# Gathering rows for a mixture of experts in two parts of 256 slots, with expert 0's products between the parts

## The chip, the cores and the metric

The kernel runs on one core of one Trainium2 chip. The metric is the device time of one execution in microseconds (us); lower is better. The core's engines are TensorE (PE, whose weight loads are listed as PEld), VectorE (DVE), ScalarE (ACT), GpSimd (POOL) and SyncE (SP), which here does little but issue transfers (DMA) from the chip's memory in its program order.

## The reference

A trunk of two layers over 256 tokens of width 1024, in float32. Each layer has a mixer (retention and chunked attention in layer 0, sliding-window attention in layer 1), then a hierarchical mixture of experts, then a gated embedding. What the change touches is the mixture:

```
g = argmax(group logits)            # one of 4 groups
top 2 of the 4 experts inside it    # 16 experts in all, two per token
act = silu(h @ w_gate[e]) * (h @ w_up[e]) * gate   # d_ff 512
out += act @ w_down[e]              # for the tokens that chose e
```

With two experts per token there are 512 token-expert pairs. Each expert has three matrices of 2 MB, 96 MB for a layer.

## The kernel before

**The mixture.** Pairs are sorted by expert into 512 slots. VectorE builds one-hot matrices PH (`gather_onehots`, tokens x slots; lines 1971 to 1974) from the slot numbers, and TensorE multiplies the normalised rows by them, which writes the rows, turned, in slot order. The rows are split in a high and a low part (HSP, `rows_split`), so that two products of a fast type give the accuracy of one. For each of the 8 steps k of the width there are 2 token tiles x 2 parts = 4 matmuls of 512 columns (line 983), 32 in a layer. The stationary operand is `HSP[part][:, t, k:D:KD]`, read with a stride of 8 elements. ScalarE and VectorE copy each product, scaled by the norm's weight, out of PSUM to XS (lines 1501, 1991). Expert e takes 64 slots from its offset on, copied to XE (`expert_rows`).

**An expert** is gate and up (`gate_up`, line 1024: 8 steps k of two matmuls, which the trace shows as 32 records; the first half is k below 4), the activation, a turn back (line 1033), down (line 1041, 16 records), and the scatter of its output with one-hots again (line 1049). From expert 2 on `step(e)` runs gate and up of e, then down of e - 1. If an expert has more than 64 rows a loop behind reloads its weights; it is not taken here.

**The order ahead of that.** In each layer TensorE gathers k = 0 to 3 of token tile 0, opens the second pair of sums (`open_sums`), gathers k = 0 to 3 of tile 1, runs the first halves of experts 0 and 1 (`first_rows`), gathers k = 4 to 7, then expert 0's second half (`other_rows(0)`), the spreads of slot numbers and gates (lines 1010 and 1012), and expert 1's second half. For expert 0 the first four k have small copies of their own of the first 64 slots (`first_block`).

**The transfers.** Weights go through nine slots of 2 MB (`weights`). A load into a slot waits for the products that read it before: halves are counted by `gate_up_halves` and `gate_up_ready`, `y_halves` and `y_ready`. All weight loads are issued by SyncE in one written order, so a load that waits holds up those behind it. The eight loads of 1 MB that follow the first three experts stand in this order for both halves:

```
for half in range(2):
    load_part(3, 1, half)   # slot of expert 0's gate
    load_part(4, 0, half)   # slot of expert 0's up
    load_part(4, 1, half)   # slot of expert 1's gate
    load_part(3, 2, half)   # slot of expert 1's up
```

Experts in WHOLE (6 to 13) load gate and up in one transfer of 2 MB each, the others in halves. Between the loads SyncE also stores the side product (the embedding's projection, `side_half_stored`) and fetches expert 2's down weight to places outside the nine slots (XD, and H by `outside`).

Of the kernel before, what the change touches and what calls it, by code (L numbers as in the profile page):

```python
# [15 lines left out]
D = 1024  # L16
# [38 lines left out]
WHOLE = (6, 14)  # L55
# [132 lines left out]
def rows_bank(k):  # L188

    return (0, 1, 4, 5, 1, 4, 1, 4)[k]  # L190
# [20 lines left out]
def build(nc, x, p, norm_mix, norm_ffn, norm_ple, final_norm, even_w_in, even_ret_gn, even_rel_bias, even_w_out,  # L211
# [6 lines left out]
    with ExitStack() as ctx:  # L218
# [196 lines left out]
        def _(sp):  # L415
# [30 lines left out]
            def experts(l, u0):  # L446
# [51 lines left out]
                for e in range(NE):  # L498
                    if e == 3:
# [173 lines left out]
        def _(pe):  # L673
# [224 lines left out]
            def experts(l, u0):  # L898
# [81 lines left out]
                def gathered_part(k, t):  # L980

                    for part in range(2):
                        mm = pe.matmul(B[rows_bank(k)][:, :], HSP[part][:, t, k:D:KD], PH[:, t, :], start=(t + part == 0),  # L983
                                       stop=(t + part == TT))
                    if t == 1:
                        mm.then_inc(sem("rows_ready"), 1)

                def gathered_first(t):

                    pe.wait_ge(sem("onehots_ready"), 2 * l + t + 1)  # L990
                    pe.wait_ge(sem("hs_low"), 3 * l + 1 + t)
                    pe.wait_ge(sem("side_copied"), 4 * l + 2)
                    for k in range(4):
                        gathered_part(k, t)

                def gathered(k, t):

                    pe.wait_ge(sem("hs_low"), 3 * l + 3)
                    if t == 0:
                        name, steps = (("rows_by_dve", 1), ("rows_by_act", 2), ("rows_by_act", 3), ("rows_by_dve", 3))[k - 4]  # L1000
                        pe.wait_ge(sem(name), 4 * l + steps)
                    gathered_part(k, t)

                def spread():

                    pe.wait_ge(sem("gates_ready"), l + 1)
                    pe.wait_ge(sem("rows_by_act"), 4 * (l + 1))
                    pe.wait_ge(sem("rows_by_dve"), 4 * (l + 1))
# [130 lines left out]
                def first_block(k):  # L1139

                    if k < 4:
                        pe.wait_ge(sem("first_block_by_dve" if k % 2 else "first_block_by_act"), 2 * l + k // 2 + 1)
                    else:
                        pe.wait_ge(sem("rows_by_dve" if k % 2 else "rows_by_act"), 4 * l + k // 2 + 1)

                def first_rows(e):

                    n = u0 + 3 * e
                    if e == 0:
                        pe.wait_ge(sem("rows_by_act"), 4 * l + 1)  # L1150
                    else:
                        pe.wait_ge(sem("xe_first"), l + 1)
                        pe.wait_ge(sem("rows_by_dve"), 4 * l + 2)
                    wait_unit(n)
                    wait_unit(n + 1)
                    gate_up(B[gu_bank(e)], XE[:, e], pair(n), None, sem("gate_up_halves"), (0,),
                            first_block if e == 0 else None)

                def other_rows(e):

                    n = u0 + 3 * e
                    if e == 1:
                        pe.wait_ge(sem("xe_ready"), NE * l + 2)
                    gate_up(B[gu_bank(e)], XS[:, :, 0:BLK] if e == 0 else XE[:, e], pair(n), lambda: wait_second(n, n + 1), None, (1,),
                            first_block if e == 0 else None).then_inc(sem("gate_up_ready"), 1)
# [12 lines left out]
                other_rows(1)  # L1178
# [189 lines left out]
        def _(act):  # L1368
# [92 lines left out]
            def experts(l, u0):  # L1461
# [21 lines left out]
                for half in range(2):  # L1483
                    seed(1, half)
# [9 lines left out]
                def first_block(k):  # L1494

                    act.wait_ge(sem("rows_ready"), 8 * l + k + 1)
                    act.activation(XE[:, 0, k], B[rows_bank(k)][:, 0:BLK], ACT.Copy, scale=NW[:, kn, k:k + 1])\
                        .then_inc(sem("first_block_by_act"), 1)

                def rows_evac(k):  # L1500
                    act.activation(XS[:, k, :], B[rows_bank(k)][:, :], ACT.Copy, scale=NW[:, kn, k:k + 1]).then_inc(sem("rows_by_act"), 1)
# [3 lines left out]
                if l == 1:  # L1505
                    act.wait_ge(sem("gate_up_ready"), NE * l - 1)
                for half in range(2):
                    for k in (4 * half, 4 * half + 2):
                        if half == 0:
                            first_block(k)  # L1510
                        else:
                            act.wait_ge(sem("rows_ready"), 8 * l + k + 1)
                        if k == 0:
                            act.wait_ge(sem("side_first_stored"), 16 * (l + 1))
                        rows_evac(k)
                    act.wait_ge(sem("rows_by_act"), 4 * l + 2 * half + 2)
                    act.wait_ge(sem("rows_by_dve"), 4 * l + 2 * half + 2)
                    rows(1, offs, slice(4 * half, 4 * half + 4), ("xe_first", "xe_ready")[half], (1, 2)[half])
                    if half == 0:
                        act.wait_ge(sem("g_below_max"), l + 1)  # L1520
                        act.activation(RT[:, 20:28], RT[:, 20:28], ACT.Exp).then_inc(sem("g_exp"), 1)
                        act.wait_ge(sem("second_below_first"), l + 1)
                        act.activation(RT[:, 84:86], RT[:, 84:86], ACT.Exp).then_inc(sem("second_exp"), 1)
# [157 lines left out]
        def _(dve):  # L1681
# [186 lines left out]
            def experts(l, u0):  # L1868
# [102 lines left out]
                for t in range(TT):  # L1971
                    then(dve.tensor_scalar(TMP[:, t, :], IOTA, S2[:, t, :], None, ALU.is_equal))
                    dve.scalar_tensor_tensor(out=PH[:, t, :], in0=IOTA, scalar=S1[:, t, :], in1=TMP[:, t, :],
                                             op0=ALU.is_equal, op1=ALU.add).then_inc(sem("onehots_ready"), 1)
# [6 lines left out]
                rows_low(1, 4, KD)  # L1981

                def first_block(k):

                    dve.wait_ge(sem("rows_ready"), 8 * l + k + 1)
                    dve.tensor_scalar(XE[:, 0, k], B[rows_bank(k)][:, 0:BLK], NW[:, kn, k:k + 1], None, ALU.mult)\
                        .then_inc(sem("first_block_by_dve"), 1)

                def rows_evac(k):

                    dve.tensor_scalar(XS[:, k, :], B[rows_bank(k)][:, :], NW[:, kn, k:k + 1], None, ALU.mult).then_inc(sem("rows_by_dve"), 1)

                if l == 1:
                    dve.wait_ge(sem("gate_up_ready"), NE * l - 1)
                first_block(1)
                dve.wait_ge(sem("side_first_stored"), 16 * (l + 1))
                rows_evac(1)
                first_block(3)
                dve.wait_ge(sem("side_second_stored"), 16 * (l + 1))
                rows_evac(3)  # L2000
# [67 lines left out]

                dve.wait_ge(sem("rows_ready"), 8 * l + 6)
                rows_evac(5)  # L2070
                dve.wait_ge(sem("rows_ready"), 8 * l + 8)
                dve.wait_ge(sem("side_third_stored"), 16 * (l + 1))
                rows_evac(7)
# [308 lines left out]
```

## Time and profile before

| | |
|---|---|
| time, median of 3 runs | 727.9 us (726.28 to 727.92) |
| the profiled execution's own time | 727.73 us |
| its span | 725.9 us |
| TensorE busy | 706.7 us, 97% |
| VectorE, ScalarE busy | 301.5 us, 166.1 us |
| transfers | 250.87 MB, mean 346 GB/s |
| granted clock of TensorE, mean | 0.994 |

In rows of windows the columns are the stretch and its length; the busy us and (in brackets) instructions of PE, PEld, DVE, ACT and POOL; the granted clock of TensorE; the share of the transfer engines; and GB/s. In rows of a timeline they are start, length to the end of the last, engine, line, operation, operands and count, and in square brackets the idle time before it and what ended that. The span is the time between the first and the last instruction of the profiled execution; 1.8 us lie around it. Each engine runs its own list of instructions and waits on semaphores. A busy engine need not be what sets the time: what counts is which wait ends last at the end of each stage.

### The profile page before, as it was taken

What the parts mean: (1) busy time and instruction counts of PE and PEld (TensorE: products, weight loads), DVE (VectorE), ACT (ScalarE), POOL (GpSimd) and SP (SyncE); (2) the same over time, 40 slices, a digit from 0 to 9 for tenths busy, and PEclk for the clock granted to TensorE, in tenths of its full rate; (3) what the DMA queues carried; (4) which work ended last, traced back from release to release, by engine and by line L of the source; (5) the groups of instructions that cost most, each with busy time, mean ns of one, the idle gap of its engine ahead of it and who ended that gap; (6) DMA issues with size and microseconds to landing.
All of it is one profiled execution on the core that took longest, in us unless ns stands there. A gap on an engine that the chain in (4) does not pass through costs nothing.

```text
span 725.9 us, 8170 instructions
## 1 busy us (share of the span) xinstructions
PE 706.7 (97%) x3062; PEld 328.4 (45%) x3062; DVE 301.5 (42%) x717; ACT 166.1 (23%) x395; POOL 26.4 (4%) x47
## 2 busy tenths in 40 slices
PE   9999999999999999989999999999999999989996
PEld 5488454564333333333445545455333333333344
DVE  1213361545437343433322557263535534324324
ACT  3000241432111111110331144252111111112132
POOL 0500000000000000000000000000000000000000
PEclk9999999999999999999999999999999999999999
DMA  9998448889999999999999851489999999999941
GB/s 344 376 285 293 184 174 328 331 310 367 421 409 424 424 431 424 426 418 422 398 381 409 328 197 79 180 284 355 412 412 426 429 422 424 428 420 422 406 164 59
DMA packets 46056, 250.87 MB, mean 346 GB/s; under 512 B 4200, under 2 KB 5448, under 8 KB 25536
## 3 DMA queue, kind: packets, MB, share of 16 engines
q1 hardware_dynamic: 43648, 245.04, 84.4%
q0 software_dynamic: 2048, 5.07, 2.2%
q8 instruction: 26, 0.43, 0.2%
q10 hardware_dynamic: 320, 0.22, 0.1%
q14 instruction: 14, 0.11, 0.0%
HBM read 247.15 MB, written 4.73 MB: 347 GB/s over the span
## 4 chain that ended last, share of the span: by engine, by line
PE 81%; DMA 9%; SPq 5%; issue 2%; DVE 2%; ACT 1%; POOLq 0%; POOL 0%; ACTq 0%; DVEq 0%
PE bank L1024 25%; PE bank L699 24%; PE bank L1041 12%; SPq L454 4%; DMA weights<-in_moe_w_up_dram 4%; PE bank L732 4%; DMA weights<-in_moe_w_down_dram 4%; PE bank L1049 3%; PE bank L983 2%; PE bank L926 2%; PE bank L684 1%; PE bank L1033 1%; DMA weights<-in_even_w_in_dram 1%; PE bank L712 1%; PE bank L770 0%
## 5 line engine op out<-in xcount | busy, mean ns | idle before, releaser
L1024 PE MATMUL bank<-weights,expert_rows 128*64 128x512 f32 x992 | 222.5, 600 | 6.2 <-DMA weights<-in_moe_w_up_dram 6.2
L699 PE MATMUL bank<-weights,normalised 128*128 128x512 f32 (+1 forms) x448 | 191.4, 580 | 0.9 <-DVE normalised L1699 0.7
L1024 PEld LDWEIGHTS bank<-weights,expert_rows 128*64 128x64 f32 x992 | 73.7, 138 | 147.1 <-issue 145.8
L699 PEld LDWEIGHTS bank<-weights,normalised 128*128 128x128 f32 x448 | 83.1, 190 | 91.4 <-issue 88.5
L1041 PE MATMUL bank<-weights,hidden_turned_odd 128*64 128x512 f32 x256 | 58.8, 598 | 0.4 <-DMA weights<-in_moe_w_down_dram 0.4
L1041 PE MATMUL bank<-weights,hidden_turned 128*64 128x512 f32 x224 | 51.5, 598 | 1.3 <-DVE hidden_turned L2029 0.6
L1534 ACT ACTIVATE gate_tanh<-bank 128x256 f32<-128x256 f32 x32 | 12.3, 384 | 175.2 <-PE bank L1024 175.2
L1385 ACT ACTIVATE expert_outputs<-bank 64x512 fp32r<-64x512 f32 (+1 forms) x32 | 18.9, 591 | 117.7 <-PE bank L1041 112.3
L2029 DVE COPY hidden_turned<-bank 128x256 f32<-128x256 f32 x16 | 6.8, 424 | 75.0 <-PE bank L1033 75.0
L2060 DVE TENSOR_TENSOR expert_outputs<-bank,expert_outputs 64x512 fp32r<-64x512 f32 x30 | 20.5, 684 | 41.7 <-ACT expert_outputs L1385 41.5
L2029 DVE COPY hidden_turned_odd<-bank 128x256 f32<-128x256 f32 x16 | 6.8, 424 | 63.3 <-PE bank L1033 63.1
L1041 PEld LDWEIGHTS bank<-weights,hidden_turned_odd 128*64 128x64 f32 x256 | 16.9, 136 | 34.8 <-issue 31.7
L2041 DVE SCALAR_TENSOR_TENSOR spread_gates<-token_slots,router_temps,token_gates 128x512 f32<-128x512 f32 x32 | 24.0, 751 | 12.9 <-ACT token_gates L1526 11.9
L1041 PEld LDWEIGHTS bank<-weights,hidden_turned 128*64 128x64 f32 x224 | 15.2, 136 | 29.2 <-issue 28.9
L732 PE MATMUL bank<-normalised,weights 128*128 128x256 f32 x128 | 28.4, 380 | 0.0
L1049 PE MATMUL bank<-expert_outputs,scatter_onehots 128*128 128x512 f32 x60 | 26.1, 436 | 0.2
L732 PEld LDWEIGHTS bank<-normalised,weights 128*128 128x128 f32 x128 | 24.1, 190 | 3.7 <-issue 0.5
L1049 PE MATMUL bank<-gather_onehots,scatter_onehots 128*128 128x512 f32 x60 | 23.6, 394 | 0.0
L2044 DVE TENSOR_REDUCE slot_gates<-spread_gates 128x1 f32<-128x512 f32 x32 | 21.9, 686 | 1.1
L1385 ACT ACTIVATE expert_rows<-normalised 128x512 f32 (+1 forms) x32 | 19.5, 611 | 10.9 <-issue 6.9
L1033 PEld LDWEIGHTS bank<-constants,hidden 128*128 128x128 f32 x64 | 10.1, 206 | 26.3 <-issue 24.7
L1381 ACT ACTIVATE normalised<-bank,norm_weights 128x128 f32<-128x128 f32 x48 | 13.7, 368 | 33.3 <-PE bank L684 33.0
(276 smaller groups left out, 647.1 us busy)
## 6 DMA issues: line engine op xcount, KB each, us to landing
weights<-in_moe_w_down_dram SPq DMA_DIRECT2D x60, 1024.0 KB, 19.6
weights<-in_moe_w_gate_dram SPq DMA_DIRECT2D x32, 1024.0 KB, 8.7
weights<-in_moe_w_up_dram SPq DMA_DIRECT2D x32, 1024.0 KB, 10.1
weights<-in_moe_w_gate_dram SPq DMA_DIRECT2D x16, 2048.0 KB, 16.5
weights<-in_moe_w_up_dram SPq DMA_DIRECT2D x16, 2048.0 KB, 21.0
weights<-in_even_w_in_dram SPq DMA_DIRECT2D x5, 2048.0 KB, 20.4
weights<-in_ple_w_gate_dram SPq DMA_DIRECT2D x4, 2048.0 KB, 31.5
weights<-in_even_w_out_dram SPq DMA_DIRECT2D x2, 2048.0 KB, 32.5
```

Source lines behind the costliest of these rows:

```text
L454: sp.dma_start(dst, src).then_inc(done, 16)
L699: mm = pe.matmul(B[bank][:, 0:width], XT[:, k, tok(t)], w[:, k, :], start=(k == 0), stop=(k == KD - 1))
L732: mm = pe.matmul(B[2 * (u % 2) + pair][:, c * SEQ:(c + 1) * SEQ], w[:, k, tok(2 * pair + c)], XT[:, k, :], start=(k == 0), stop=(k == KD - 1))
L926: mm = pe.matmul(B[4 + 2 * t + half][:, :], PINT[:, k, tok(t)], WPL[k][:, half * 512:(half + 1) * 512], start=(k == 0), stop=(k == 1))
L1024: mm = pe.matmul(bank[j * BLK:(j + 1) * BLK, :].rearrange("p (m f) -> p m f", m=2), rows[:, k, :], W[:, slots, a:a + FF // 2], start=(k == ...
L1033: mm = pe.transpose(B[TURNED_BANK][:, c * P:(c + 1) * P], US[:, c:2 * P:2], ident)
L1041: mm = pe.matmul(bank[half * BLK:(half + 1) * BLK, :], hid[:, 2 * (f % 2) + f // 2, :], rows(f)[:, half * 512:(half + 1) * 512], start=(f ...
L1049: return pe.matmul(B[sum_bank(t, half)][:, :], PT2[:, par, tok(t)], YSPLIT[half][:, par, :], start=False, stop=stop)
L1385: return act.activation(dst, src, ACT.Copy)
L2041: stepped(dve.scalar_tensor_tensor(out=SPREAD, in0=SROW.rearrange("p c s -> p (c s)"), scalar=col, in1=WROW.rearrange("p c s -> p (c s)"), ...
L2044: stepped(dve.tensor_reduce(GATES[:, par:par + 1], SPREAD, AX.X, ALU.add), gates)
L2060: return dve.tensor_tensor(YSPLIT[half][low, par, :], bank[high, :], YSPLIT[half][high, par, :].bitcast(F32), ALU.subtract)
```

## The change

The gather is divided by slots instead of by k. First TensorE gathers slots 0 to 255 for all eight k (32 matmuls of 256 columns), then runs expert 0's whole gate and up, reading its rows from XS, then gathers slots 256 to 511 (32 more), then expert 1's first half, the spreads, and expert 1's second half. Two k share a PSUM bank. The one-hots are built for 256 slots at a time, with the low part of the rows of tile 1 between. `first_block` goes. ScalarE copies k = 0, 1, 4, 5 and VectorE k = 2, 3, 6, 7 of each part, 256 wide. ScalarE seeds the second pair of sums behind its first two copies. SyncE stores the last quarter of the side product ahead of the 1 MB load of expert 2's down weight, not behind it. WHOLE becomes 8 to 13, so experts 6 and 7 load gate and up in halves, in the branch `elif e != 4`: first halves of both, then second halves, then down of the expert before. The order of the other loads is as it was.

```diff
-WHOLE = (6, 14)
+WHOLE = (8, 14)
...
-def rows_bank(k):
-    return (0, 1, 4, 5, 1, 4, 1, 4)[k]
+def rows_bank(half, k):
+    return ((0, 1, 4, 5), (5, 4, 1, 4))[half][k // 2]
+def in_bank(k):
+    return slice(256 * (k % 2), 256 * (k % 2) + 256)
+def evac_count(half, k):
+    return 4 * half + 2 * (k // 4) + k % 2 + 1
...
# SyncE
                         side_half_stored(0)
-                        sp.wait_ge(sem("side_ready"), 4 * l + 4)
+                        sp.wait_ge(sem("side_copied"), 4 * l + 4)
+                        side_half_stored(1)
                         sp.dma_start(XD[:, :], srcs[2][l * NE + 2][0:256, :].rearrange("(p c) d -> p (c d)", c=2))\
                             .then_inc(sem("down2_landed"), 16)
-                        sp.wait_ge(sem("side_copied"), 4 * l + 4)
-                        side_half_stored(1)
...
# TensorE
+                def gathered(half, k):
+                    for t in range(TT):
+                        for part in range(2):
+                            mm = pe.matmul(B[rows_bank(half, k)][:, in_bank(k)], HSP[part][:, t, k:D:KD],
+                                           PH[:, t, 256 * half:256 * half + 256], start=(t + part == 0), stop=(t + part == TT))
+                    mm.then_inc(sem("rows_ready"), 1)
+                def gathered_first():
+                    pe.wait_ge(sem("onehots_ready"), 4 * l + 2)
+                    pe.wait_ge(sem("hs_low"), 3 * l + 2)
+                    pe.wait_ge(sem("side_copied"), 4 * l + 2)
+                    for k in range(4):
+                        gathered(0, k)
+                    pe.wait_ge(sem("side_copied"), 4 * l + 4)
+                    open_sums(1)
+                    pe.wait_ge(sem("hs_low"), 3 * l + 3)
+                    for k in range(4, KD):
+                        gathered(0, k)
+                def gathered_second():
+                    pe.wait_ge(sem("onehots_ready"), 4 * l + 4)
+                    for k in range(KD):
+                        if k == 0:
+                            pe.wait_ge(sem("rows_by_dve"), 8 * l + evac_count(0, 7))
+                        elif k == 2:
+                            pe.wait_ge(sem("rows_by_act"), 8 * l + evac_count(0, 5))
+                        elif k == 6:
+                            pe.wait_ge(sem("rows_by_dve"), 8 * l + evac_count(1, 3))
+                        gathered(1, k)
...
-                gathered_first(0)
-                pe.wait_ge(sem("side_copied"), 4 * l + 4)
-                open_sums(1)
-                gathered_first(1)
-                first_rows(0)
-                first_rows(1)
-                for k in range(4, KD):
-                    for t in range(TT):
-                        gathered(k, t)
-                other_rows(0)
+                gathered_first()
+                first_expert()
+                gathered_second()
+                second_expert(0)
                 spread()
-                other_rows(1)
+                second_expert(1)
...
# ScalarE
+                act.wait_ge(sem("side_first_stored"), 16 * (l + 1))
+                rows_evac(0, 0)
+                rows_evac(0, 1)
+                for half in range(2):
+                    seed(1, half)
+                act.wait_ge(sem("onehots_ready"), 4 * l + 4)
+                rows_evac(0, 4)
+                rows_evac(0, 5)
...
+                for part in range(2):
+                    rows_evac(1, 4 * part)
+                    rows_evac(1, 4 * part + 1)
+                    act.wait_ge(sem("rows_by_act"), 8 * l + evac_count(1, 4 * part + 1))
+                    act.wait_ge(sem("rows_by_dve"), 8 * l + evac_count(1, 4 * part + 3))
+                    rows(1, offs, slice(4 * part, 4 * part + 4), ("xe_first", "xe_ready")[part], (1, 2)[part])
...
# VectorE
+                gather_onehots(0)
+                rows_low(1, 4, KD)
+                gather_onehots(1)
...
+                rows_evac(0, 2)
                 dve.wait_ge(sem("side_second_stored"), 16 * (l + 1))
-                rows_evac(3)
+                rows_evac(0, 3)
+                rows_evac(0, 6)
+                dve.wait_ge(sem("side_third_stored"), 16 * (l + 1))
+                rows_evac(0, 7)
...
+                for k in (2, 3, 6, 7):
+                    rows_evac(1, k)
```

## Rows read from the trace of the kernel before

**Rows 1.** The page: TensorE busy, and the transfers' share by slice

```profile
PE 706.7 (97%) x3062; PEld 328.4 (45%) x3062; DVE 301.5 (42%) x717; ACT 166.1 (23%) x395; POOL 26.4 (4%) x47
...
DMA  9998448889999999999999851489999999999941
```

**Rows 2.** Waits of TensorE: us in total, times, longest

```profile
PE bank L1024 <- DMA weights<-in_moe_w_up_dram: 6.2, 4, 2.7
```

**Rows 3.** Windows: engines' busy us, granted clock, transfers' share, GB/s

```profile
210.00:222.00 12.00, 12.00 (x58) 4.34 (x56) 5.08 (x11) 2.20 (x4) 0.00 (x0) 1.00 0.97 410
...
246.00:258.00 12.00, 12.00 (x58) 4.32 (x56) 5.04 (x11) 2.21 (x4) 0.00 (x0) 1.00 1.01 425
...
310.00:314.00 4.00, 2.66 (x8) 0.92 (x10) 0.73 (x2) 0.00 (x0) 0.00 (x0) 0.65 1.01 420
```

**Rows 4.** Timeline of TensorE, ends of both layers' experts: start, length in us

```profile
311.34 8.71 PE L1024 MATMUL bank<-weights,expert_rows 128*64 128x512 f32 x32 [2.72 <-DMA weights<-in_moe_w_up_dram]
...
351.34 1.94 PE L1041 MATMUL bank<-weights,hidden_turned_odd 128*64 128x512 f32 x8 [0.42 <-DMA weights<-in_moe_w_down_dram]
...
682.53 3.85 PE L1041 MATMUL bank<-weights,hidden_turned_odd 128*64 128x512 f32 x16
```

**Rows 5.** Timeline of TensorE, layer 0, from the first gather

```profile
146.74 2.51 PE L983 MATMUL bank<-gather_onehots,rows_split 128*128 128x512 f32 x8
...
151.87 7.09 PE L1024 MATMUL bank<-weights,expert_rows 128*64 128x512 f32 x32
...
158.89 4.69 PE L983 MATMUL bank<-gather_onehots,rows_split 128*128 128x512 f32 x16
...
163.50 3.65 PE L1024 MATMUL bank<-weights,normalised 128*64 128x512 f32 x16
...
169.07 3.65 PE L1024 MATMUL bank<-weights,expert_rows 128*64 128x512 f32 x16
```

**Rows 6.** Timeline of SyncE's queue (SPq), loads of experts 3 and 4

```profile
155.56 0.33 SPq L454 DMA_DIRECT2D weights<-in_moe_w_up_dram  x1
...
159.00 0.33 SPq L454 DMA_DIRECT2D weights<-in_moe_w_up_dram  x1
...
167.20 0.33 SPq L454 DMA_DIRECT2D weights<-in_moe_w_up_dram  x1
...
172.76 0.33 SPq L454 DMA_DIRECT2D weights<-in_moe_w_up_dram  x1
...
492.64 0.33 SPq L454 DMA_DIRECT2D weights<-in_moe_w_up_dram  x1
```

**Rows 7.** Windows of 22 and of 2 us, same columns

```profile
154.00:176.00 22.00, 21.20 (x100) 10.78 (x98) 8.94 (x26) 4.90 (x10) 0.00 (x0) 1.00 0.86 326
...
696.00:698.00 2.00, 2.00 (x6) 0.95 (x5) 0.15 (x1) 1.64 (x5) 0.09 (x1) 1.00 0.50 207
```

**Rows 8.** Timeline of the weight loads (PEld), in short windows

```profile
147.14 1.80 PEld L983 LDWEIGHTS bank<-gather_onehots,rows_split 128*128 128x128 f32 x7
...
158.88 0.31 PEld L983 LDWEIGHTS bank<-gather_onehots,rows_split 128*128 128x128 f32 x1 [0.81 <-issue]
...
159.10 0.59 PEld L983 LDWEIGHTS bank<-gather_onehots,rows_split 128*128 128x128 f32 x2
```

**Rows 9.** Groups by line: count, busy us, mean ns of one

```profile
L983 PEld LDWEIGHTS bank<-gather_onehots,rows_split 128*128 128x128 f32 x64 | 16.5, 329 | 3.3 <-issue 2.4 <-DVE gather_onehots L1973 0.5
...
L1049 PEld LDWEIGHTS bank<-expert_outputs,scatter_onehots 128*128 128x128 f32 x60 | 11.5, 192 | 3.4 <-issue 2.2
```

**Rows 10.** The chain that ended last: start us, us, what

```profile
184.96 0.93 PE bank L1049 x4
...
379.42 0.88 PE bank L684 x8
```

**Rows 11.** Timeline of VectorE, the slots' selection, layer 0

```profile
145.37 0.49 DVE L1972 TENSOR_SCALAR normalised<-normalised,router_temps 128x512 f32<-128x512 f32 x1
...
147.07 0.75 DVE L1973 SCALAR_TENSOR_TENSOR gather_onehots<-normalised,router_temps 128x512 fp32r<-128x512 f32 x1
```

More of the change, by code:

```diff
@@ L978, in experts @@
                 side_part(1, 1, 1)
[L980 to L991, printed above, removed]
+                def gathered(half, k):
[4 more added lines that the diff above has]
+                    mm.then_inc(sem("rows_ready"), 1)
@@ L1170, in experts, with row_in_place, first_expert @@
-                gathered_first(1)
-                first_rows(0)
-                first_rows(1)
-                for k in range(4, KD):
-                    for t in range(TT):
-                        gathered(k, t)
-                other_rows(0)
+                def row_in_place(k):
+                    pe.wait_ge(sem("rows_by_act" if by_act(k) else "rows_by_dve"), 8 * l + evac_count(0, max(k, 1)))
+                def first_expert():
+                    wait_unit(u0)
+                    wait_unit(u0 + 1)
+                    gate_up(B[gu_bank(0)], XS[:, :, 0:BLK], pair(u0), lambda: wait_second(u0, u0 + 1), sem("gate_up_halves"),
+                            row_ready=row_in_place).then_inc(sem("gate_up_ready"), 1)
@@ new lines, in second_expert @@
+                def second_expert(half):
+                    n = u0 + 3
+                    if half == 0:
+                        pe.wait_ge(sem("xe_first"), l + 1)
+                        pe.wait_ge(sem("rows_by_act"), 8 * l + evac_count(1, 1))
+                        wait_unit(n)
+                        wait_unit(n + 1)
+                        gate_up(B[gu_bank(1)], XE[:, 1], pair(n), None, sem("gate_up_halves"), (0,))
+                    else:
+                        pe.wait_ge(sem("xe_ready"), NE * l + 2)
+                        gate_up(B[gu_bank(1)], XE[:, 1], pair(n), lambda: wait_second(n, n + 1), None, (1,))\
+                            .then_inc(sem("gate_up_ready"), 1)
@@ L1482, in experts @@
                             seed(0, half)
-                for half in range(2):
-                    seed(1, half)
                 def rows(e, off=None, part=slice(0, KD), done="xe_ready", count=1):
@@ L1492, in rows, with rows_evac @@
                     copy(XE[:, e % 2, part], XS[:, part, bass.ds(off, BLK)]).then_inc(sem(done), count)
[L1494 to L1501, printed above, removed]
+                def rows_evac(half, k):
+                    act.wait_ge(sem("rows_ready"), 16 * l + 8 * half + k + 2 - k % 2)
+                    act.activation(XS[:, k, 256 * half:256 * half + 256], B[rows_bank(half, k)][:, in_bank(k)], ACT.Copy,
+                                   scale=NW[:, kn, k:k + 1]).then_inc(sem("rows_by_act"), 1)
@@ new lines, in experts @@
+                act.wait_ge(sem("side_first_stored"), 16 * (l + 1))
[6 more added lines that the diff above has]
+                rows_evac(0, 5)
+                act.wait_ge(sem("g_below_max"), l + 1)
+                act.activation(RT[:, 20:28], RT[:, 20:28], ACT.Exp).then_inc(sem("g_exp"), 1)
+                act.wait_ge(sem("second_below_first"), l + 1)
@@ L1503, in experts @@
+                act.activation(RT[:, 84:86], RT[:, 84:86], ACT.Exp).then_inc(sem("second_exp"), 1)
                 act.wait_ge(sem("table_ready"), 2 * l + 1)
                 offs = act.value_load(TBL[0:1, 1:2], min_val=0, max_val=LAST)
[L1505 to L1523, printed above, removed]
@@ L1970, in experts, with gather_onehots @@
                 dve.wait_ge(sem("iota_ready"), 2 * (l + 1))
[L1971 to L1974, printed above, removed]
+                def gather_onehots(half):
+                    c = slice(256 * half, 256 * half + 256)
+                    for t in range(TT):
+                        then(dve.tensor_scalar(TMP[:, t, c], IOTA[:, c], S2[:, t, :], None, ALU.is_equal))
+                        dve.scalar_tensor_tensor(out=PH[:, t, c], in0=IOTA[:, c], scalar=S1[:, t, :], in1=TMP[:, t, c],
+                                                 op0=ALU.is_equal, op1=ALU.add).then_inc(sem("onehots_ready"), 1)
+                gather_onehots(0)
+                rows_low(1, 4, KD)
+                gather_onehots(1)
                 one = slice(0, 1)
```

54 lines of the change are left out of this document (8 added, 46 removed).

## The prediction

> **What bounds the kernel now.** I read the page first. TensorE is busy 97% of the span, and the transfers run at nine tenths or more in most slices [rows 1], so shares alone decide nothing. The waits of TensorE for transfers sum to only 6.2 us in four waits [rows 2]. Read alone, that says TensorE is the bound. The windows and the timeline say otherwise for the expert stretches. From about 174 us to the end of layer 0's experts the transfers move 410 to 425 GB/s at a share of 0.97 to 1.01 [rows 3], and at the end TensorE waits 0.42 us for the second half of the last down weight before it can do the last 8 matmuls at 351.34 [rows 4]. An expert takes TensorE some 11.8 us and the transfers 3 x 2.10 MB at 0.424 MB/ns, 14.8 us. TensorE eats up a lead of filled slots, starts to wait at the twelfth expert or so, and the layer ends when its last weight lands. That is a chain of transfers that runs without a gap back to about 173 us. So the question for the change is what it does to the transfers in the 30 us ahead of that, where the queue still runs dry: 154 to 176 us moved 326 GB/s [rows 7].
>
> What starts transfers there? SyncE issues in program order, and each of four pairs of 1 MB waits for a slot: pair A for expert 0's first half of gate and up, pair B for expert 1's first half, pair C for expert 0's second half, pair D for expert 1's second. They go at 155.6, 159.0, 167.2 and 172.8 [rows 6]. The timeline of TensorE shows the causes: first halves of experts 0 and 1 together from 151.87 to 158.9, then gathers, expert 0's second half from 163.50, then the spreads, expert 1's second half from 169.07 [rows 5].
>
> **The change part by part.**
>
> *Gathers, 32 of 512 columns become 64 of 256 in each layer.* The price is the spacing of such matmuls. Now seven weight loads of the gather take 1.80 us, the last 0.33: (1.80 - 0.33)/6 = 0.245 us from one to the next [rows 8]. The scatters, also 128x512 out of fp32r operands, are spaced at 0.93/4 = 0.232 [rows 10]. The difference lies in the load: 0.330 us each in the gather, whose stationary rows are read at a stride of 8, against 0.192 in the scatter [rows 9]. And after a gap, with no matmul streaming, the gather's first load starts at 158.88 and its second at 159.10 [rows 8]: 0.22 us for a load by itself. So the gather's spacing today is the load's, not the 512 columns', and half the columns save next to nothing. I take 0.24; bounds are 0.22 (a bare load) and 0.245, and as the far end 0.11, at which the transposes of 128 columns run (0.87/8) [rows 10], if the load turned out to be no limit. At 0.24, 32 gathers are 7.7 us.
>
> The Trainium skill, in "TensorE: Matmul & The Clock Gate", section "LDWEIGHTS (loading the stationary operand)", gives a load as its columns over 1.2, 107 ns for 128, and its section "Back-to-back issue gap" gives 256 columns 109 ns. By the page's figures 32 gathers would be 3.5 us and the whole about 731 us. By that rule, the trace disagrees: 0.22 to 0.245 us lie between its loads.
>
> *The order.* The start stays: the side product holds TensorE until 147.1 [rows 8]. Selecting the slots takes VectorE from 145.37 to 147.8 now for both token tiles [rows 11]; half as wide, four operations take between half of that and all of it, so the gather starts between 147.1 and 147.8; I take 147.1. Then:
> first gather 7.7, and 0.4 for opening two sums: 155.2;
> expert 0 whole, twice the 3.5 us of 16 matmuls [rows 5]: 162.2, its first half at 158.7;
> second gather 7.7 and 0.2 for its first load: 170.1;
> expert 1's first half 3.6: 173.7;
> spreads 2.0, second half 3.6: 179.3.
> Today expert 1's first half ends at 158.9, the spreads at 169.1 and its second half at 172.7 [rows 5]. So expert 0 is whole 5 us earlier (167.1 to 162.2), its first half 3.3 us later, expert 1's first half 14.8 us later and its second 6.6 later. TensorE alone is 6.6 us later from here on, 7.7 of gathers less some gaps.
>
> *The transfers.* Pair A goes at 158.8. Pair B must wait for 173.7, and pair C, free since 162.2, stands behind it in SyncE's queue. It then goes at once, D at 179.3. Pair A lands within some 1.5 us (issue to data) plus 2.10/0.424 = 4.9 us, at about 165, and then nothing moves for 9 us. From 173.7 on the queue stays full, as it does now from 172.8. But at that point today A, B and C are done, and then only A is. The transfers are behind by two pairs and 0.9 us: 2 x 4.9 + 0.9 = 10.8 us. A little of it can come back where they run below their best today (410 against 425 GB/s in 210 to 222 us [rows 3], 0.4 us): 10.4.
>
> *What hides it.* Nothing at layer 0's end: TensorE already waits there [rows 4], so the end moves by 10.4. TensorE's own 6.6 us lie inside. What was some 3.1 us of waits in the layer, half of the 6.2, becomes about 7. An idle stretch also lowers the clock: 310 to 314 us has a granted clock of 0.65 [rows 3] after the 2.72 us wait, a mix of 2.4 and 1.2 GHz, and the 32 matmuls there take 8.71 us [rows 4] for 7.0. There is room for that under 14.8 us an expert, so I cost it at nothing, 1.7 us where the cover fails at the last expert.
>
> Layer 1 has the same order at an offset of 333.6 us (pair B at 492.64 [rows 6]) and pays the same 10.4. At its end the last 16 matmuls run without a wait [rows 4], so there is slack. The transfers end at about 697 [rows 7]; after the last down weight come 5.8 MB (two gates, side product, a row), 14 us, so it lands at 683.0 and its matmuls start at 684.4. Slack 1.4: layer 1 moves by 9.0.
>
> *The small parts.* Evacuations become 256 wide and twice as many. The eight of the first part lie beside the 7 us of expert 0, where ScalarE and VectorE have no other product to fetch; in the second part matmuls 6 and 7 reuse a bank that VectorE empties two copies (under 0.75 us each) before, beside 2 us of gathers; a stall of 0 to 1 us. The eight small copies of expert 0's rows go (under 0.3 us each, beside gathers): nothing. Seeding the second sums moves behind two evacuations, so the 0.5 MB load that waits for it goes about 1.6 us later, the 1 MB one 1 us later; both land before 158.8 in a queue that is dry anyway. Expert 6 and 7 in halves ask for each slot's half earlier; with the queue full that reorders bytes and starts nothing: 0, at best the 0.4 us above once more.
>
> **Sum.** 10.4 + 9.0 = 19.4 us on the profiled execution's 727.7 (span 725.9 and 1.8 around it): 747.1. That execution stands 0.2 below the median of the runs, 727.9. I say 747.
>
> **Rivals.**
> A, short gathers: the load is no limit at 256 columns, spacing 0.11. Then expert 1's first half ends at 158.4 + 64 x 0.11 = 165.4 and pair B is late by less; the lag is that end less 162.9 (173.7 less 10.8), 2.5 us, less the slack in layer 1: 2.5 + 1.1 = 3.6, 731 us. For it: half the columns. Against it: the 0.22 us between bare loads.
> B, the lag is partly made up: the transfers catch up and TensorE's 6.6 us set each end, less waits of today: 5 to 6 us a layer, 739. It needs 450 GB/s over 177 us; the windows show 425.
> C, the other side: pair C 5 us earlier wins. It decides only where pair B, ahead of it in SyncE's order, goes before 162.9, which needs a spacing under (162.9 - 158.4)/64 = 0.07 us. At 0.05, as for half the time of a 128-column transpose, the lag is -1.3 a layer: 725. No row has such a spacing.
> D, no effect: a spacing of about 0.07, 728.
>
> **Numbers.** My forecast 0.76, A 0.10, B 0.07, C 0.04, D 0.03. Its own range: spacing 0.22 takes 64 x 0.02 = 1.3 us a layer off, 744.5; start at 147.8, a stall of 1 us and a cold last expert in both layers put 0.7 + 1 + 0.5 a layer on, 751.5. With B the range is 738 to 752, which leaves A, C and D out. A difference under 0.3% (2.2 us) can't be told from none here. Faster 0.04, same 0.03, slower 0.93.
>
> **What would show it.** In the trace after: 128 gather matmuls spaced at 0.24 us with loads still of 0.33; in SyncE's timeline a single pair near 158.8 and then nothing until about 173.7, when four 1 MB loads go within 2 us; in the windows from 166 to 174 a transfer share near 0; TensorE's waits for transfers up from 6 us to about 14, the first at expert 11 or 12; the same in layer 1. Wrong it would be if the gathers' spacing fell to 0.12 (A), or if the lag at 174 us were not there any more at the last down weight (B).

## The result, and the profile after

| | before | after |
|---|---|---|
| time, median of 4 runs, taken in turn | 727.91 us (726.28 to 729.18) | 748.52 us (747.97 to 748.98) |
| the profiled execution's own time | 727.73 us | 748.98 us |
| its span | 725.9 us | 747.2 us |

The ratio is 1.028, with a 95% interval of 1.026 to 1.031: slower, by 20.6 us between the medians. The forecast was 747 us. Medians and ratios below leave out the few executions that stood far above the rest of their kernel (782.69 us once in 12, and 815 to 1871 us three times among those of the kernel before).

The page of the kernel after, its span, busy times, transfers in 40 slices, and the gather's groups:

```profile
span 747.2 us, 8320 instructions
PE 722.4 (97%) x3126; PEld 345.9 (46%) x3126; DVE 303.2 (41%) x729; ACT 167.2 (22%) x399; POOL 26.4 (4%) x47
DMA  9998349865999999999999760665999999999941
L998 PEld LDWEIGHTS bank<-gather_onehots,rows_split 128*128 128x128 f32 x128 | 31.2, 336 | 3.3 <-issue 2.1
L998 PE MATMUL bank<-gather_onehots,rows_split 128*128 128x256 f32 x128 | 32.4, 409 | 0.0
```

TensorE is busy 97% of a span that is 21 us longer: the share says nothing, as before [rows 1]. A load of the gather's stationary rows takes 336 ns, about as it did [rows 9], and there are twice as many. The slices, each 18.7 us long, show the place. In the ninth and tenth, 149 to 187 us, the transfers' share is six and five tenths, where the ninth and tenth of before, 145 to 181 us, have eight and nine [rows 1]. In layer 1 the 27th and 28th, 486 to 523 us, have six and five.

The timeline of TensorE, from the first gather in layer 0 (it answers to [rows 5]):

```profile
147.70 4.13 PE L998 MATMUL bank<-gather_onehots,rows_split 128*128 128x256 f32 x16
...
152.17 4.11 PE L998 MATMUL bank<-gather_onehots,rows_split 128*128 128x256 f32 x16
156.21 7.09 PE L1047 MATMUL bank<-weights,normalised 128*64 128x512 f32 x32
163.23 7.97 PE L998 MATMUL bank<-gather_onehots,rows_split 128*128 128x256 f32 x32
171.13 3.65 PE L1047 MATMUL bank<-weights,expert_rows 128*64 128x512 f32 x16
...
176.70 3.65 PE L1047 MATMUL bank<-weights,expert_rows 128*64 128x512 f32 x16
```

The second gather is 32 matmuls in 7.97 us; less the last one's 0.41 that is 7.56/31 = 0.244 us each. Expert 1's first half ends at 174.8.

SyncE's queue, the loads of experts 3 and 4 (it answers to [rows 6]):

```profile
159.91 0.33 SPq L469 DMA_DIRECT2D weights<-in_moe_w_up_dram  x1
...
174.83 0.33 SPq L469 DMA_DIRECT2D weights<-in_moe_w_up_dram  x1
...
175.67 0.43 SPq L469 DMA_DIRECT2D weights<-in_moe_w_up_dram  x1
...
180.39 0.33 SPq L469 DMA_DIRECT2D weights<-in_moe_w_up_dram  x1
...
503.50 0.33 SPq L469 DMA_DIRECT2D weights<-in_moe_w_up_dram  x1
...
518.42 0.33 SPq L469 DMA_DIRECT2D weights<-in_moe_w_up_dram  x1
```

Pair A stands alone at 159.91, pair B goes at 174.83, pair C right behind it, D at 180.39; layer 1 repeats it. The windows say what that costs (it answers to [rows 7]):

```profile
154.00:176.00 22.00, 22.00 (x101) 14.41 (x101) 5.52 (x25) 3.77 (x10) 0.00 (x0) 1.00 0.39 137
166.00:174.00 8.00, 8.00 (x36) 6.06 (x37) 1.75 (x4) 1.99 (x5) 0.00 (x0) 1.00 0.08 32
```

The stretch of 22 us moved 326 GB/s before and moves 137 now; in 166 to 174 us almost nothing is under way, while TensorE works without a gap.

The waits of TensorE for transfers, and its timeline at the ends of the layers (they answer to [rows 2] and [rows 4]):

```profile
PE bank L1047 <- DMA weights<-in_moe_w_up_dram: 11.4, 8, 2.7
...
PE bank L1064 <- DMA weights<-in_moe_w_down_dram: 0.9, 2, 0.5
```

```profile
292.63 7.09 PE L1047 MATMUL bank<-weights,expert_rows 128*64 128x512 f32 x32 [0.70 <-DMA weights<-in_moe_w_up_dram]
...
361.90 1.94 PE L1064 MATMUL bank<-weights,hidden_turned_odd 128*64 128x512 f32 x8 [0.47 <-DMA weights<-in_moe_w_down_dram]
...
705.71 1.94 PE L1064 MATMUL bank<-weights,hidden_turned_odd 128*64 128x512 f32 x8 [0.46 <-DMA weights<-in_moe_w_down_dram]
```

The sum is 12.3 us, the first wait of layer 0 is at expert 11 (292.63), and both layers now end on a wait for the last down weight. By stages, from the starts of such rows (us):

| stage | before | after | more |
|---|---|---|---|
| start to layer 0's first gather | 146.7 | 147.7 | 1.0 |
| to the last half of layer 0's last down | 204.6 | 214.2 | 9.6 |
| to layer 1's first gather | 129.1 | 129.4 | 0.3 |
| to the last half of layer 1's last down | 204.0 | 214.4 | 10.4 |
| to the end of the span | 41.4 | 41.4 | 0 |

### The profile page after: what moved, and what is told of

Same layout as the page of the kernel before. It is cut to its first block, busy times and chain, and to the rows that moved or that the text cites. A ratio compares the mean times of both kernels' runs of the same rounds, so it can differ in the third digit from the quotient of the medians.

```text
span 747.2 us, 8320 instructions
## 1 busy us (share of the span) xinstructions
PE 722.4 (97%) x3126; PEld 345.9 (46%) x3126; DVE 303.2 (41%) x729; ACT 167.2 (22%) x399; POOL 26.4 (4%) x47
## 4 chain that ended last, share of the span: by engine, by line
PE 69%; DMA 15%; SPq 10%; issue 2%; DVE 2%; ACT 1%; POOLq 0%; POOL 0%; ACTq 0%; DVEq 0%
PE bank L713 24%; PE bank L1047 17%; SPq L469 10%; DMA weights<-in_moe_w_up_dram 8%; PE bank L1064 7%; DMA weights<-in_moe_w_down_dram 7%; PE bank L998 4%; PE bank L746 4%; PE bank L940 2%; PE bank L1072 2%; PE bank L698 2%; PE bank L726 1%; PE bank L1056 1%; PE bank L852 1%; PE bank L784 0%
## 5 line engine op out<-in xcount | busy, mean ns | idle before, releaser
L1047 PE MATMUL bank<-weights,expert_rows 128*64 128x512 f32 x960 | 215.8, 601 | 11.4 <-DMA weights<-in_moe_w_up_dram 11.4
L1047 PEld LDWEIGHTS bank<-weights,expert_rows 128*64 128x64 f32 x960 | 72.7, 139 | 147.1 <-issue 146.6
L1542 ACT ACTIVATE gate_tanh<-bank 128x256 f32<-128x256 f32 x32 | 12.3, 384 | 181.3 <-PE bank L1047 181.3
L998 PEld LDWEIGHTS bank<-gather_onehots,rows_split 128*128 128x128 f32 x128 | 31.2, 336 | 3.3 <-issue 2.1
L998 PE MATMUL bank<-gather_onehots,rows_split 128*128 128x256 f32 x128 | 32.4, 409 | 0.0
L1399 ACT ACTIVATE expert_rows<-normalised 128x512 f32 (+1 forms) x32 | 19.5, 611 | 15.3 <-issue 10.9
```

The source lines that it names most:

```text
L998: mm = pe.matmul(B[rows_bank(half, k)][:, in_bank(k)], HSP[part][:, t, k:D:KD], PH[:, t, 256 * half:256 * half + 256], start=(t + part == ...
L1047: mm = pe.matmul(bank[j * BLK:(j + 1) * BLK, :].rearrange("p (m f) -> p m f", m=2), rows[:, k, :], W[:, slots, a:a + FF // 2], start=(k == ...
L1399: return act.activation(dst, src, ACT.Copy)
```

## Experiments

Each ratio is to the kernel before, run in turn with it on the same chip. Stages are read from one profiled execution each, and kernels that do the same in a stage differ there by up to 1.4 us.

### Only the wait, without the gathers

The kernel before, with pair B, and so all that stands behind it, held until the second half of expert 1 is done (`gate_up_ready` counts experts whose gate and up are whole):

```diff
                             load_part(4, 0, half)
+                            if half == 0:
+                                sp.wait_ge(sem("gate_up_ready"), NE * l + 2)
                             load_part(4, 1, half)
```

> The kernel before, with one wait added to SyncE: pair B waits for expert 1's second half (172.8 us in layer 0) instead of its first (159.0), so pairs B, C and D go together. TensorE gets no work. Theory 1, the chain of transfers sets each layer's end: at 174.3 us, when pair D's data starts now, two pairs are missing, 9.9 us; less 1.4 us of slack at the end of layer 1 the time is 727.9 + 9.9 + 8.5 = 746 us (743 to 748). Theory 2, TensorE's own 6.6 us per layer set the end of the changed kernel, and a gap in the transfers is made up before a layer ends: 728 us, at most 731.

744.61 us, ratio 1.025 (1.023 to 1.026). No instruction of TensorE was added or moved. SyncE's queue, the windows and the waits of this kernel:

```profile
155.66 0.33 SPq L454 DMA_DIRECT2D weights<-in_moe_w_up_dram  x1
...
172.84 0.33 SPq L454 DMA_DIRECT2D weights<-in_moe_w_up_dram  x1
```

```profile
154.00:176.00 22.00, 21.20 (x100) 10.77 (x98) 8.93 (x27) 4.90 (x10) 0.00 (x0) 1.00 0.39 135
...
200.00:230.00 30.00, 30.00 (x142) 10.63 (x140) 15.43 (x43) 5.59 (x10) 0.00 (x0) 1.00 1.01 425
```

```profile
PE bank L1026 <- DMA weights<-in_moe_w_up_dram: 19.3, 11, 2.7
```

At 172.84 pairs B, C and D go one behind another, where before only D was left: two pairs behind. That alone lengthens the expert stages by 8.1 and 8.9 us. So the stall of the transfers by itself makes a loss of nearly the size of the change's, and over 180 us little of it is caught up, where rival B wanted about half. TensorE, with less to do than in the kernel after, just waits longer: 19.3 us. The stall is not given back in full, but a little is: 9.8 us went in, 8.1 and 8.9 came out. From 200 to 230 us this kernel moves 425 GB/s where before moved 415 (its window is among those below): 0.7 us of that.

### Pair C ahead of pair B

The kernel after, with the pairs in the order in which their slots come free:

```diff
                         for half in range(2):
                             load_part(3, 1, half)
                             load_part(4, 0, half)
+                        for half in range(2):
                             load_part(4, 1, half)
                             load_part(3, 2, half)
```

> The changed kernel with pair C (free at about 163 us) issued ahead of pair B (free at about 175). TensorE's work is as in the changed kernel. Theory 1: one pair of 2.1 MB lands in the gap of the transfers, so the lag is 4.9 us less in each layer: 748.5 - 9.9 = 738.6 us (737 to 741). Theory 2: TensorE's added work is unchanged, so is the time: 748.5 us (747 to 750).

740.43 us, ratio 1.019 (1.017 to 1.021). SyncE's queue and two windows:

```profile
158.83 0.33 SPq L469 DMA_DIRECT2D weights<-in_moe_w_up_dram  x1
...
162.26 0.33 SPq L469 DMA_DIRECT2D weights<-in_moe_w_up_dram  x1
...
173.75 0.33 SPq L469 DMA_DIRECT2D weights<-in_moe_w_up_dram  x1
...
179.31 0.33 SPq L469 DMA_DIRECT2D weights<-in_moe_w_up_dram  x1
```

```profile
176.00:180.00 4.00, 3.75 (x18) 1.18 (x14) 3.02 (x7) 2.04 (x6) 0.00 (x0) 1.00 0.91 377
...
180.00:182.00 2.00, 1.44 (x8) 0.70 (x10) 1.93 (x5) 0.59 (x1) 0.00 (x0) 1.00 1.00 352
```

Pair C, which now goes 11.5 us ahead of pair B, wins 4.0 and 3.9 us in the two stages, about the 4.9 us of a pair. So 8 of the 20 us were the head of the queue: a load whose slot was free stood behind one whose slot was not. The rest of the 4.9: between B at 173.75 and D at 179.31 a single pair is under way, and the windows run at 377 and 352 GB/s, not 424, which is 0.4 + 0.3 us.

### What the gather's spacing is made of

Two ways to store the split rows so that the stationary operand is contiguous. In the first ScalarE and VectorE read the rows at a stride of 8; in the second they write them at a stride of 128 elements, and VectorE also reads the high part back at that stride. TensorE's line is the same in both. The edits are shortened here to VectorE's views; ScalarE's copy of the high part changes in the same way:

```diff
-  HSP[part][:, t, k:D:KD]
+  HSP[part][:, t, k * P:(k + 1) * P]
 # first: split kept as (k, m), rows read as (m, k)
+  cols      = lambda ap: ap.rearrange("p (k m) -> p k m", k=KD)[:, a:b, :]
+  wide_cols = lambda ap: ap.rearrange("p (m k) -> p k m", k=KD)[:, a:b, :]
 # second: rows read in order, split written as (m, k) into (k, m)
+  cols      = lambda ap: ap.rearrange("p (k m) -> p m k", k=KD)[:, :, a:b]
```

Contiguous, read at a stride, in the kernel after:

> The changed kernel, with the split rows stored in the order of k (written so by ScalarE and VectorE, read by the same count of elements), so that a gather's stationary operand is contiguous. Theory 1, the strided weight load spaces the gathers: the load falls from 0.33 to 0.19 us, the spacing from 0.25 to 0.12 or 0.13, expert 1's first half ends 8 us earlier, and the time is 731 to 735 us, 733 likeliest. Theory 3, a gather matmul costs 0.25 us for another reason (its issue, its type, the PSUM side): spacing and time stay, 748 us. If the strided reads in ScalarE and VectorE cost, the start of the gather is later by up to 1 us in each layer.

737.48 us, ratio 1.015 (1.013 to 1.018). The timeline of TensorE, and groups by line:

```profile
147.92 2.18 PE L998 MATMUL bank<-gather_onehots,rows_split 128*128 128x256 f32 x16
...
159.56 4.44 PE L998 MATMUL bank<-gather_onehots,rows_split 128*128 128x256 f32 x32
```

```profile
L998 PEld LDWEIGHTS bank<-gather_onehots,rows_split 128*128 128x128 f32 x128 | 15.8, 191 | 3.9 <-issue 2.1 <-DVE gather_onehots L1986 1.2 <-DVE normalised L2002 0.6
...
L1885 DVE SCALAR_TENSOR_TENSOR rows_split<-residual,norm_stats,rows_split 128x512 fp32r<-128x512 f32 (+1 forms) x6 | 8.9, 1478 | 8.5 <-ACT rows_split L1482 8.5
...
L1482 ACT ACTIVATE rows_split<-residual,norm_stats 128x1024 fp32r<-128x1024 f32 x4 | 8.6, 2161 | 0.0
```

The load falls from 336 to 191 ns and 32 matmuls from 7.97 to 4.44 us, 0.13 us each. The same 256 columns are now nearly half as dear: the stride in the load was the limit, not the columns. But the price goes elsewhere. ScalarE's pass over a tile of the rows rises from 1161 ns to 2161, VectorE's from 923 to 1478 on the mean, and the stage between the layers is 132.0 us, 2.9 more than before. Of the expert stages 2.2 and 2.6 us are left over before's. The time is 2.5 us above the range expected: the strided passes cost 1.2 us ahead of layer 0 and 2.9 between the layers, where up to 1 us a layer was allowed for.

Contiguous, written at a stride, the same kernel otherwise:

> The changed kernel with the split rows in the order of k by strided writes instead of strided reads. The stage between the layers took 132.0 us with strided reads against 129.1; the stages from the first gather to the last down product were 206.8 and 206.6. If writes at a stride are free: 129.1 between the layers and 737.5 - 4.2 = 733 us. If they cost the same: 737.5.

737.49 us, ratio 1.013 (1.011 to 1.015). ScalarE's pass takes 2.08 us: written or read at a stride, the price is the same.

The second way with pair C first:

> The changed kernel with both repairs: split rows in the order of k, this time read as they lie and written at a stride of 128 elements, and pair C issued ahead of pair B. By theory 1 the gathers are spaced at 0.13 us, pairs A, C, B, D go at about 155.5, 159, 167 and 172.5 us, against 155.6, 159.0, 167.2 and 172.8 for the four pairs of the kernel before: pair D's data starts 0 to 0.5 us earlier in each layer, 727 us (726 to 728.5), if the strided writes are free. If they cost as the strided reads did (3 us ahead of layer 1, 1.2 ahead of layer 0), 731 us.

730.35 us, ratio 1.004 (1.002 to 1.005). The expert stages are 203.4 and 204.4 us, those of before within what a stage varies; the 2.5 us left stand ahead of layer 0 (0.8) and between the layers (2.6), where the strided passes are, less the 0.8 gained in the expert stages.

### The 512-column gather with contiguous rows

The second way in the kernel before, nothing else changed:

> The kernel before, 512-column gathers, with the split rows in the order of k by strided writes. The spacing goes from 0.245 to the scatters' 0.232, set by the columns and no more by the load: 0.4 us a layer for TensorE, pairs C and D up to 0.3 us earlier, 726.5 us if the writes are free, about 731 if not. If the load were no limit at 512 columns either, the spacing would stay at 0.245.

730.46 us, ratio 1.004 (1.002 to 1.005): slower, though TensorE spends less on the gathers (16.5 us of loads become 11.4). The 16 gathers ahead of expert 0's second half take 4.29 us for 4.69 [rows 5]:

```profile
159.43 4.29 PE L983 MATMUL bank<-gather_onehots,rows_split 128*128 128x512 f32 x16
```

Between the starts of such matmuls lie 0.233 us for 0.247 (medians). So contiguous, 512 columns are spaced at 0.23 us and 256 at 0.13; at a stride of 8 both are at about 0.245. TensorE's timeline between the layers, of this kernel and then of before:

```profile
469.38 0.40 PE L913 MATMUL bank<-constants,router_temps 128*128 128x20 f32 x2 [1.82 <-DVE router_temps L1884]
469.62 3.66 PE L699 MATMUL bank<-weights,normalised 128*128 128x512 f32 x4
```

```profile
468.10 0.40 PE L913 MATMUL bank<-constants,router_temps 128*128 128x20 f32 x2 [0.22 <-DVE router_temps L1882]
468.35 1.96 PE L699 MATMUL bank<-weights,normalised 128*128 128x512 f32 x4
```

ScalarE's pass and then VectorE's, 0.9 and 0.7 us longer, stand ahead of VectorE's copy of the router's logits, so TensorE waits 1.82 us for 0.22, and the four matmuls behind take 3.66 us for 1.96. The granted clock over 461 to 481 us is 0.91 here and 1.00 before. 1.6 us of wait and 1.7 of the slower clock make most of the 3.9 us by which the stage between the layers is longer (133.0 for 129.1).

Could the longer pass be hidden? VectorE copies the logits ahead of the low part of tile 0, and makes that of tile 1 behind the ranking:

```diff
-                rows_low(0)
                 logits_moved(0)
+                rows_low(0)
...
-                rows_low(1, 0, 4)
                 compared(1)
                 ranked(1)
+                rows_low(1, 0, 4)
```

> The kernel before with contiguous stationary rows (strided writes), and on VectorE the low part of the rows behind the copy of the logits for token tile 0 and behind the routing's comparisons for tile 1, so that ScalarE's longer split (2.08 us for 1.16) no longer stands ahead of the routing. If the 3.9 us lost between the layers came by that wait (1.82 us of TensorE idle, then four matmuls in 3.66 us for 1.96 at the lower clock), it goes, and the gain of 1.1 us in each layer's stage stays: 725.5 us (724.5 to 726.5). If the loss came by something else: about 730 us.

727.55 us, ratio 0.999 (0.998 to 1.001). The wait for the logits is gone and 3 us with it, but another has come, and the time is 2 us above the one expected:

```profile
470.88 1.16 PE L684 MATMUL bank<-constants,residual 128*128 128x128 f32 x8 [1.38 <-DVE residual L1706]
```

The residual's sum is now what stands behind the 2.0 us pass. The same order with the strided load of before, as a control:

> The kernel before with only that order on VectorE. There the wait of TensorE for the logits' copy is 0.22 us and TensorE stays at the full clock: 727.5 us, at best 0.7 us gained.

727.58 us, ratio 1.000 (0.999 to 1.001). And with the change's order of gathers and experts and pair C first:

> The changed kernel with all three: contiguous rows, pair C ahead of pair B, the low part later on VectorE. The stages took 203.4 and 204.4 us against 204.6 and 204.0 before; with the 2.6 us between the layers back, 727.5 us (726 to 728.5), no more than the kernel before. By theory 1 the order of the change has then no advantage left, since pair D, which ends the dry stretch, goes at 172.8 in both.

727.70 us, ratio 1.000 (0.999 to 1.001). With the spacing and the queue mended, and most of the price of the split's stride hidden (the stage between the layers is 130.2 us, 1.1 over before), the change's order ties with before and wins nothing. No version here beats it.

### The halves of experts 6 and 7

The kernel before with WHOLE = (8, 14), and the kernel after with WHOLE = (6, 14):

> The kernel before with gate and up of experts 6 and 7 in halves, and nothing else of the change. With the queue full there it starts no byte earlier or later: 727.9 us within 1 us. If instead the finer transfers bring back what 204 to 222 us lose (397 and 410 GB/s against 425), 0.8 us a layer: 726.3. If four more transfers in SyncE's order hold up others, slower by up to 2 us.

726.89 us, ratio 1.000 (0.999 to 1.001).

> The changed kernel with experts 6 and 7 whole again (WHOLE from 6). The transfers run at 422 to 425 GB/s there with the lag anyway: 748.5 us within 1.5 us, and pair B still at about 174. If the halves mattered here, more than 1.5 us off.

747.75 us, ratio 1.027 (1.025 to 1.029), against 1.028 (1.026 to 1.031) for the change whole. The windows of 200 to 230 us, of before and then of before with halves:

```profile
200.00:230.00 30.00, 30.00 (x140) 10.66 (x138) 15.44 (x44) 5.59 (x10) 0.00 (x0) 1.00 1.00 415
```

```profile
200.00:230.00 30.00, 30.00 (x140) 10.70 (x138) 15.47 (x42) 5.59 (x10) 0.00 (x0) 1.00 1.02 425
```

What halves win there, 0.7 us, doesn't stand out in the time: the medians differ by 0.2 us, in the other direction by 0.8 in the kernel after, both inside what runs differ.

## Why the prediction was right, point by point

**The gather.** Put at 0.24 us a matmul because the load, not the columns, was taken for the limit; measured 0.244. Rival A said 0.11. The contiguous load shows both the reason and the rival's one merit: without the stride it is 0.13, and the kernel stands at 737.5 with the dearer passes of the split in it. Rivals C and D needed a spacing of 0.07 or less, which no kernel showed; with pair C put first and the load contiguous the order of the change comes to the time of before, as D had it, but by two edits that the change doesn't have. The 107 ns that follow for a load of 128 columns from the Trainium skill ("TensorE: Matmul & The Clock Gate", "LDWEIGHTS (loading the stationary operand)") are near that 0.13 us, and that section says nothing of a stride.

**The order and the queue.** Pairs A to D were put at 158.8, 173.7, at once behind, and 179.3; they went at 159.9, 174.8, 175.7 and 180.4. Of that 1.1 us, 0.6 is the start: the first gather was put at 147.1, or 147.8 at the latest, and stood at 147.70, where its load had waited 0.60 us for the one-hots of both tiles (0.24 before). The rest lies in the first gather and the opening of two sums, 8.5 us (147.70 to 156.21) for 8.1. Against before the start is 1.0 us later, but it is not certain that this is the change's: the kernel with pair C first, the same up to there and with the same wait of 0.60 us, began its gather at 146.6. The transfers' share of 0.08 from 166 to 174 us is the predicted gap. Pair A landed at 167.4, 7.5 us behind its issue, where 6.4 was put; nothing in the sum rests on that.

**The lag.** One sum, put together after the runs, fits the four kernels within 1.7 us: pairs still to go when the queue fills for good, at 4.9 us, and how much later that is, counted from the first gather. Before it is 26.0 us from the first gather to pair D. In the kernel after pair B goes at 27.1 with two more pairs to move: 1.1 + 9.8 = 10.9.

| kernel | late by | pairs behind | in, us | out, layer 0 | out, layer 1 |
|---|---|---|---|---|---|
| after | 1.1 | 2 | 10.9 | 9.6 | 10.4 |
| pairs held, gathers as before | 0.0 | 2 | 9.8 | 8.1 | 8.9 |
| pair C first | 1.1 | 1, and a gap of 0.7 | 6.7 | 5.6 | 6.5 |
| contiguous load (pair B at 167.63) | -6.3 | 2 | 3.5 | 2.2 | 2.6 |

Out of each 0.2 to 1.7 us is missing, 1.0 on the mean, where the prediction allowed 0.4. The windows account for 0.5 to 0.7 us of it (422 and 425 GB/s from 200 to 230 us where before moved 415); the rest stays unexplained, at the size by which a stage varies. The rows behind the -6.3 and the 422 are these, of the kernel with the contiguous load and of the kernel after:

```profile
167.63 0.33 SPq L469 DMA_DIRECT2D weights<-in_moe_w_up_dram  x1
```

```profile
200.00:230.00 30.00, 30.00 (x140) 11.03 (x138) 11.61 (x23) 5.43 (x10) 0.00 (x0) 1.00 1.02 422
```

The prediction asked more of rival B than it needs: 450 GB/s over 177 us would make up the whole lag, half of it needs about 437. The runs moved 422 to 425, so B falls all the same.

**The mis-sized term.** Layer 1 was put at 10.4 less a slack of 1.4; it moved by 10.4. There was no slack, and the trace of before could have said so. That "the last 16 matmuls run without a wait" was read from a row of TensorE that groups them, 3.85 us long [rows 4], where 16 such take 3.65. The weight loads of before in the same place:

```profile
683.39 0.14 PEld L1041 LDWEIGHTS bank<-weights,hidden_turned_odd 128*64 128x64 f32 x2 [0.29 <-issue]
684.44 0.20 PEld L1041 LDWEIGHTS bank<-weights,hidden_turned_odd 128*64 128x64 f32 x4 [0.91 <-DMA weights<-in_moe_w_down_dram]
```

The last eight matmuls' loads waited 0.91 us for the down weight, of which 0.2 reached TensorE. The landing time of 683.0, worked back over 14 us from the end of the transfers, was 1.4 us off. So layer 1 of before was bound by transfers too. The sum against the spans: 1.0 + 9.6 + 0.3 + 10.4 = 21.3 us, for 19.4 predicted: the missing slack and the later start, less what came back. That these errors partly cancel is luck; the larger part, two pairs behind in each layer, is not.

**The rest.** Waits for transfers 12.3 us (about 14 predicted), the first at expert 11 (11 or 12 predicted). Experts 6 and 7 in halves: nothing, as put. Evacuations, the seeding and the moved store were costed at nothing; they were not tried one by one, but the 32 matmuls of the second gather run in 7.97 us without a gap, so the stall of up to 1 us for a bank did not come.

## What to carry to other kernels

Where transfers are issued in one written order, the slots must come free in that order: before moving work on the compute engine, list for each load when its slot comes free, and look for the first that would block others; here it turned 6.6 us of added TensorE time in a layer into a delay of some 10, 20 us in all, and putting the loads in another order gave back 8. What sets a matmul's spacing may be its load, so cutting columns gives nothing until the load's stride is gone; and a stride taken from one engine must be paid by another, whose cover has to be looked up first. To tell slack at a stage's end, read the weight loads one by one: a grouped row hides a short wait.

## What the runs showed of the hardware

A load of 128x128 with a stride of 8 elements of 4 bytes takes 329 to 337 ns, contiguous 188 to 191, and the spacing of matmuls of 256 columns goes from 0.244 to 0.13 us. Strides cost the other engines about as much: passes over 128x1024 take ScalarE 1.16 us in order and 2.07 to 2.16 with one side strided, VectorE 1.28 and 1.96 to 2.09, whether it is the read by 8 or the write by 128 elements (there VectorE reads one operand by 128 as well). The Trainium skill has a reason that would fit, in "SBUF — State Buffer", in a note of its section on "Door 1: The DMA port swizzle": lines of 16 bytes, with at least two accesses to a line needed for the full rate, so strides up to 4 elements of 4 bytes are free. By that rule, the trace agrees: both strides are beyond it. A stride of 2 or 4 was not tried.

Waits of TensorE of the same length had a slower clock behind them in some executions and not in others. These are the same place in three kernels: contiguous and written at a stride, in the order of the change; the same with pair C first; and rows read at a stride.

```profile
473.46 0.40 PE L927 MATMUL bank<-constants,router_temps 128*128 128x20 f32 x2 [1.82 <-DVE router_temps L1892]
473.71 2.78 PE L713 MATMUL bank<-weights,normalised 128*128 128x512 f32 x4
```

```profile
469.32 0.40 PE L928 MATMUL bank<-constants,router_temps 128*128 128x20 f32 x2 [1.80 <-DVE router_temps L1893]
469.57 1.96 PE L714 MATMUL bank<-weights,normalised 128*128 128x512 f32 x4
```

```profile
473.27 0.40 PE L927 MATMUL bank<-constants,router_temps 128*128 128x20 f32 x2 [2.00 <-DVE router_temps L1892]
473.52 1.96 PE L713 MATMUL bank<-weights,normalised 128*128 128x512 f32 x4
```

In the first, as in the 512-column kernel above (3.66 us behind 1.82), the granted clock over 461 to 481 us is 0.91; in the other two it is 1.00. Behind a wait of 1.38 us between the layers and one of 1.17 us among the experts (at 322.21 in the kernel after) the matmuls ran at their full rate too. The length of the wait alone didn't decide it, and about 1 us of the stage between the layers (133.0 us with the slower clock, 132.0 and 131.7 without) hangs on it.
